# Requesting the modulation's weights from ScalarE's queue instead of SyncE's in a two-layer encoder kernel

## Chip, cores and metric

The kernel runs on one core of a Trainium2 chip. The metric is the device time of one launch in microseconds (us). The core has five engines with an instruction queue each: TensorE (PE; its weight loads are listed as PEld), VectorE (DVE), ScalarE (ACT), GpSimd (POOL) and SyncE (SP). Sixteen DMA engines move data between the memory outside the core and the on-chip buffers; an instruction on SP, ACT or POOL asks for a transfer.

## The reference

The program computes one inference step of a trunk of two layers on 384 rows of 2048 numbers: 256 rows of one new stream and 16 rows of each of 8 running streams. Each layer first makes three vectors for each of the 9 streams from a conditioning vector `c`. This is the **modulation**; its weights are a matrix of 2048 by 6144 for each layer, all in float32:

```
def modulate(x, c, norm_g, w_mod, b_mod):
    mod = jax.nn.silu(c) @ w_mod + b_mod
    shift, scale, gate = jnp.split(mod, 3, axis=-1)
    h = rms_norm(x, norm_g) * (1 + scale[:, None, :]) + shift[:, None, :]
    return h, gate[:, None, :]
...
    for l in range(DEPTH):
        h, gate = modulate(x, c, norm_g[l], w_mod[l], b_mod[l])
        ...  # even layer: spatial gating beside retention; odd layer: gated linear attention
        x = x + gate * y
```

The shift and scale of a layer are wanted before the layer's projections, its gate only after them. So of the modulation the kernel needs one third before anything of the first layer can start (shift and scale of layer 0 are two of six equal parts), and the other four parts (gate of layer 0; shift, scale and gate of layer 1) much later.

## The kernel before

**Granules.** Every big product is done in float32 accuracy with three products of a high and a low part. Weights come in granules of 256 by 512 numbers (512 KB). A granule goes through four hands: SP asks for it (`load_main`, line 391) into one of four `raw` buffers; ACT copies its high part to `whi` (`split_main`, line 775, the instruction at line 783); DVE subtracts to get the low part `wlo` (line 1133); PE multiplies it with three tiles of rows (`granule`, line 1715), which is 18 matmuls. ACT's `split_main(n)` waits until PE is through with granule n - 4 (the semaphore `w_used`, which starts at `LEAD` = 16), because there are four `whi` and `wlo` buffers. SP's `load_main(n)` waits until DVE has made the low part of granule n - 4 (`lo_ready`).

**The stretch that the change touches.** Granules 0 to 127 belong to the spatial gating of layer 0: four heads of 24 granules (three panels of 8: v, u and z) and, after each two heads, four output panels of 4 granules. Granules from 128 on belong to retention and to layer 1 and are loaded by another function (`load`, line 377, its DMA at line 389).

**The modulation's later parts.** Four parts (`GROUP`, i = 0 to 3) of 16 batches each make 64 batches, numbered `nb` from 32 on (0 to 31 are the first stage, `load_batch`, line 400). A batch is two transfers of 512 KB into one of two buffers (`SLOT` is 1 or 2 in turn; the buffers are the four `state` tiles, which the retention uses later). PE takes batches in pairs at 32 **places** between granules (`PLACE`, `group_batch`, line 1777: eight matmuls a batch in the trace, named `turn<-state,cT`, and one count on `mod_used`). A place lies behind some granule N: behind the 4th and 8th granule of a panel (every four granules), in one panel, the z panel of head 0, behind every second, and behind the last granule of each output panel. The table `BEHIND` says at which granule's load the pair for a place is asked for, two granules after N:

```
BEHIND[ph * (N_GM // 2) + 24 * (h % 2) + 8 * p + g + 2] += [nb, nb + 1]
...
BEHIND[min(ph * (N_GM // 2) + 48 + 4 * pn + 5, N_GM - 1)] += [nb, nb + 1]
```

In the kernel before, SP walks this table in `load_main`: behind its request for granule n it calls `load_group(nb)` (line 412, DMA at line 419) for the pair listed there. `load_group` waits on `mod_used` until PE has used the batch that was last in the same buffer, so until the place before, and everything later on SP's queue waits behind it. SP's requests are all on one hardware DMA queue (q1 in the profile); POOL's are on another (q0).

Of the kernel before, what the change touches and what calls it, by code (L numbers as in the profile page):

```python
# [34 lines left out]
W = 512  # L35
# [16 lines left out]
N_GM = 128  # L52
# [5 lines left out]
GROUP = [(0, 8), (1, 0), (1, 4), (1, 8)]  # L58
# [3 lines left out]
BEHIND = {n: [] for n in range(N_GM)}  # L62
for ph in range(2):
    for h in (2 * ph, 2 * ph + 1):
        for p in range(3):
            for g in ((), (3, 7), (1, 3, 5, 7))[IN_HEAD[h][p] // 4]:
                nb = NBATCH * N_FIRST + 2 * len(PLACE)
                PLACE["head", h, p, g] = (nb, nb + 1)
                BEHIND[ph * (N_GM // 2) + 24 * (h % 2) + 8 * p + g + 2] += [nb, nb + 1]
    for pn in range(4):  # L70
        nb = NBATCH * N_FIRST + 2 * len(PLACE)
        PLACE["out", ph, pn] = (nb, nb + 1)
        BEHIND[min(ph * (N_GM // 2) + 48 + 4 * pn + 5, N_GM - 1)] += [nb, nb + 1]
SLOT = [nb % 5 if nb < NBATCH * N_FIRST else 1 + nb % 2 for nb in range(N_BATCH)]
TURN = [SLOT[:nb].count(SLOT[nb]) for nb in range(N_BATCH)]
LAST = [max([-1] + [n for n in range(nb) if SLOT[n] == SLOT[nb]]) for nb in range(N_BATCH)]
# [13 lines left out]
def build(nc, a, consts, outs):  # L90
# [6 lines left out]
    w_m = [a["w_mod"][l].rearrange("(k p) n -> p k n", p=P) for l in range(2)]  # L97
# [4 lines left out]
    with ExitStack() as ctx:  # L102
# [6 lines left out]
        def sem(name):  # L109
            return ctx.enter_context(nc.semaphore(name))  # L110
# [30 lines left out]
        def carve(at, *shape):  # L141

            v = work[:, at:at + int(np.prod(shape))]
            if len(shape) == 2:
                v = v.rearrange("p (a b) -> p a b", a=shape[0])
            if len(shape) == 3:
                v = v.rearrange("p (a b c) -> p a b c", a=shape[0], b=shape[1])
            return v
# [7 lines left out]
        MT = [(raw[1][:, :, :], raw[3][:, :, :])] + [  # L156
            tuple(state[c][:, :].rearrange("p (k n) -> p k n", k=GK) for c in (2 * i, 2 * i + 1)) for i in range(2)] + [
            (carve(1536, GK, W), carve(3584, GK, W)), (carve(4608, GK, W), carve(5760, GK, W))]
# [64 lines left out]
        s = {n: sem(n) for n in names}  # L223
# [3 lines left out]
        mod_in = [sem(f"mod_in{k}") for k in range(len(MT))]  # L227
# [3 lines left out]
        def at_least(eng, sm, n):  # L231

            if not isinstance(n, int) or n > 0:
                eng.wait_ge(sm, n)
# [16 lines left out]
        def main_slot(n):  # L251

            return n - N_GM if n >= N_GM else (1, 3, 0, 2)[n % 4] if n >= 8 else 2 * (n % 2)

        def main_raw(n):

            return raw[main_slot(n)][:, :, :]

        def main_turn(n):

            return sum(main_slot(m) == main_slot(n) for m in range(n + 1))

        def group_of(nb):

            return (nb - NBATCH * N_FIRST) // KT, (nb - NBATCH * N_FIRST) % KT
# [92 lines left out]
        def nothing(*_):  # L358
            pass
# [16 lines left out]
        def _(sp):  # L376
# [14 lines left out]
            def load_main(n, src):  # L391

                if n in (8, 9):
                    sp.wait_ge(s["mod_used"], max(nb for nb in range(N_FIRST * NBATCH) if SLOT[nb] == 0) + 1)
                else:
                    at_least(sp, s["lo_ready"], n - 1 if n < 8 else n - 3)
                sp.dma_start(main_raw(n), src).then_inc(main_in[main_slot(n)], 16)
                for nb in BEHIND[n]:
                    load_group(nb)

            def load_batch(q, b):

                nb, p = NBATCH * q + b, PANEL[q]
                at_least(sp, s["mod_used"], LAST[nb] + 1)
                if nb == 3:
                    sp.wait_ge(s["cT_full"], 1)
                for i in range(2):
                    k = 4 * b + 2 * i
                    sp.dma_start(MT[SLOT[nb]][i], w_m[0][:, k:k + GK, p * W:p * W + W])\
                        .then_inc(mod_in[SLOT[nb]], 16)  # L410

            def load_group(nb):

                i, k = group_of(nb)
                layer, p = GROUP[i]
                sp.wait_ge(s["mod_used"], LAST[nb] + 1)
                for q in range(2):
                    c0 = (p + 2 * q) * W
                    sp.dma_start(MT[SLOT[nb]][q], w_m[layer][:, k, c0:c0 + 2 * W].rearrange("p (j n) -> p j n", j=2))\
                        .then_inc(mod_in[SLOT[nb]], 16)  # L420

            def panel(r, src):
# [8 lines left out]
            def gmlp_main(h, n0, p, g):  # L431
                c0 = (D, 0, 2 * D)[p] + h * W
                load_main(n0 + 8 * p + g, w_e[:, GK * g:GK * g + GK, c0:c0 + W])

            def modulation():
                for m in range(8):
                    for b in range(NBATCH):
                        if m % 2 == 0 and m >= 2 and b == 3:
                            gmlp_main(0, 0, 0, m - 2)
                        if m % 2 and m >= 3 and b == 1:  # L440
                            gmlp_main(0, 0, 0, m - 2)
                        load_batch(m, b)
# [6 lines left out]
            def gm_out(ph, pn, n, ai, yi, oi, before):  # L449
                for g in range(4):  # L450
                    k = ph * 8 + GK * g
                    load_main(n + g, wo[0][:, k:k + GK, pn * W:pn * W + W])
# [309 lines left out]
        def _(act):  # L762
# [12 lines left out]
            def split_main(n):  # L775

                if n >= N_GM:
                    act.wait_ge(raw_in[n - N_GM], 32)
                else:
                    act.wait_ge(main_in[main_slot(n)], 16 * main_turn(n))  # L780
                if n >= NSLOT:
                    act.wait_ge(s["w_used"], n - NSLOT + 1 + LEAD)
                act.activation(whi[n % NSLOT][:, :, :], main_raw(n), ACT.Copy).then_inc(s["hi_ready"], 1)  # L783

            def start():
                act.wait_ge(s["cT_full"], 1)
                act.activation(cth, SC[:, 0:KT * NC9].rearrange("p (k c) -> p k c", k=KT), ACT.Tanh,
                               scale=0.5).then_inc(s["th_done"], 1)
                act.wait_ge(s["vec_full"], 1)
                act.activation(vecT, OB[0][:, 0:P], ACT.Copy).then_inc(s["vec_done"], 1)  # L790
# [29 lines left out]
            def modulation():  # L820
                panel_out(0)
                for m in range(2, 8):
                    k0 = 4 * (m // 2 - 1)
                    if m % 2 == 0:
                        panel_out(m - 1)
                        act.wait_ge(s["sel_done"], m)
                        for k in (k0, k0 + 1, k0 + 2):
                            prompt(0, k)
                            high(0, k)
                        if m in (4, 6):  # L830
                            act.wait_ge(s["wsT_full"], m // 2 - 1)
                            act.activation(wsT_all[:, :, m // 2 - 2, :],
                                           OB[0][:, :].rearrange("p (h t) -> p h t", h=A_HEADS),
                                           ACT.Copy).then_inc(s["wsT_done"], 1)
                        panel_out(m)
                        split_main(m - 2)
                    else:
                        prompt(0, k0 + 3)
                        high(0, k0 + 3)
                        split_main(m - 2)  # L840
                panel_out(7)
                act.wait_ge(s["sel_done"], 8)
                for g in (6, 7):
                    prompt(0, 2 * g)
                    prompt(0, 2 * g + 1)
                    high(0, 2 * g)
                    high(0, 2 * g + 1)
                    split_main(g)
# [1457 lines left out]
```

## Time and profile before

| | |
|---|---|
| Median of 3 runs | 2734.3 us (2734.03 to 2734.69) |
| The profiled execution | 2733.85 us, of which the span of the trace is 2732.3 us |
| PE busy | 2674.1 us (98% of the span) |
| DVE, ACT, POOL busy | 1277.0, 880.1, 522.9 us |
| Mean DMA rate | 192 GB/s |
| TensorE clock granted | 0.992 of full speed (below it only near the start) |

The page has the busy time of each engine, the span in 40 slices, the DMA queues, the chain of work that ended last, and the costliest groups of instructions. Other views of the trace list who waited for whom, the instructions in order of time, and the time from a DMA's issue to its landing. Times inside the trace count from the span's start.

### The profile page before, as it was taken

Reading aid. Unit: us, or ns where it says so; the run is one execution under the profiler, and the core shown is the slowest. Engines: PE = TensorE matmul, PEld = TensorE weight load, DVE = VectorE, ACT = ScalarE, POOL = GpSimd, SP = SyncE. Lnnn points to the kernel's source line nnn. Section 1 sums busy time; section 2 is a strip of 40 time slices with the busy share of each in tenths; the row PEclk is TensorE's granted clock in tenths of the full one; section 3 lists DMA queues with packets and bytes.
Section 4 is the critical chain, followed back from the end, with each engine's and each line's share of the span. In section 5 each row is a group of like instructions: output and inputs, shape, how many; then the busy total and the mean of one; then the engine's idle time right before and its main releaser. Section 6 shows DMA issues by size and latency. Waiting matters only on the chain.

```text
span 2732.3 us, 36512 instructions
## 1 busy us (share of the span) xinstructions
PE 2674.1 (98%) x13257; PEld 2059.0 (75%) x13257; DVE 1277.0 (47%) x1849; ACT 880.1 (32%) x1241; POOL 522.9 (19%) x622
## 2 busy tenths in 40 slices
PE   6999999999999999999999999999999999999998
PEld 3677777777788888888877777786868777786866
DVE  2334343334444545455555464544554463544656
ACT  1423222222222332232323534422434334422431
POOL 3201030002311103111123121231122120231113
PEclk8999999999999999999999999999999999999999
DMA  9867676667654446455554364545556364655454
GB/s 374 316 247 260 227 252 226 228 215 235 217 178 143 157 158 211 129 173 179 169 161 126 101 231 144 199 150 185 163 182 195 117 230 140 203 159 185 157 190 154
DMA packets 280707, 523.78 MB, mean 192 GB/s; under 512 B 26593, under 2 KB 125041, under 8 KB 280041
## 3 DMA queue, kind: packets, MB, share of 16 engines
q1 hardware_dynamic: 240498, 389.17, 43.1%
q0 software_dynamic: 40064, 132.69, 14.2%
q8 instruction: 90, 1.47, 0.2%
q14 instruction: 55, 0.45, 0.1%
HBM read 460.78 MB, written 60.96 MB: 191 GB/s over the span
## 4 chain that ended last, share of the span: by engine, by line
PE 90%; issue 3%; DMA 2%; DVE 2%; POOL 1%; ACT 1%; SPq 0%; DVEq 0%; POOLq 0%; ACTq 0%
PE acc L1713 76%; PE turn L1713 6%; PE scores L1713 3%; PE mixed L1713 3%; DMA work<-in_w_mod 1%; DMA state<-in_w_mod 1%; POOL work L571 1%; DVE state L1665 1%; PE turn L1880 0%; DMA raw<-in_w_in_e 0%; POOL small L534 0%; POOL out L656 0%; PE mixed L1880 0%; PE turn L2120 0%; PE turn L2033 0%
## 5 line engine op out<-in xcount | busy, mean ns | idle before, releaser
L1713 PE MATMUL acc<-whi,hT_hi 128*128 128x512 f32 x2496 | 988.2, 396 | 5.8 <-POOL hT_lo L709 1.8
L1713 PE MATMUL acc<-whi,hT_lo 128*128 128x512 f32 x2496 | 973.6, 390 | 0.0
L1713 PE MATMUL acc<-wlo,hT_hi 128*128 128x512 f32 x2496 | 973.3, 390 | 0.0
L1122 DVE TENSOR_TENSOR wlo<-raw,whi 128x1024 fp32r<-128x1024 f32 x413 | 524.1, 1277 | 602.7 <-ACT whi L769 602.2
L769 ACT ACTIVATE whi<-raw 128x1024 fp32r<-128x1024 f32 x413 | 435.8, 1059 | 922.2 <-PE acc L1713 908.4
L1713 PEld LDWEIGHTS acc<-whi,hT_hi 128*128 128x128 f32 x2496 | 469.2, 188 | 153.0 <-issue 51.0
L1713 PEld LDWEIGHTS acc<-whi,hT_lo 128*128 128x128 f32 x2496 | 469.0, 188 | 100.3
L1713 PEld LDWEIGHTS acc<-wlo,hT_hi 128*128 128x128 f32 x2496 | 469.5, 188 | 93.2
L1133 DVE TENSOR_TENSOR wlo<-raw,whi 128x1024 fp32r<-128x1024 f32 x131 | 166.7, 1277 | 318.5 <-ACT whi L783 317.6
L1713 PE MATMUL acc<-whi,yT_hi 128*128 128x512 f32 x768 | 301.7, 393 | 7.1 <-DVE work L1381 3.7
L1713 PE MATMUL acc<-wlo,yT_hi 128*128 128x512 f32 x768 | 299.8, 390 | 0.0
L1713 PE MATMUL acc<-whi,yT_lo 128*128 128x512 f32 x768 | 299.5, 390 | 0.0
L783 ACT ACTIVATE whi<-raw 128x1024 fp32r<-128x1024 f32 x131 | 137.3, 1057 | 328.5 <-PE acc L1713 272.2
L617 POOL TENSOR_TENSOR x<-x,work 128x512 f32 (+1 forms) x90 | 140.0, 1581 | 316.5 <-DVE work L1381 311.1
L1713 PEld LDWEIGHTS acc<-whi,yT_hi 128*128 128x128 f32 x768 | 144.4, 188 | 46.3 <-issue 7.6
L1713 PEld LDWEIGHTS acc<-whi,yT_lo 128*128 128x128 f32 x768 | 144.6, 188 | 30.5
L1713 PEld LDWEIGHTS acc<-wlo,yT_hi 128*128 128x128 f32 x768 | 144.6, 188 | 29.6
L571 POOL TENSOR_TENSOR work<-work 128x512 f32<-128x512 f32 (+1 forms) x54 | 76.3, 1431 | 261.7 <-DVE work L1292 244.7
L1665 DVE SCALAR_TENSOR_TENSOR state<-state,work,turn 128x512 f32<-128x512 f32 x64 | 45.0, 745 | 168.2 <-PE mixed L1713 168.2
L656 POOL DMA_DIRECT2D out<-state x96 | 71.6, 745 | 180.3 <-DVE state L1665 146.3
L1713 PE MATMUL mixed<-work 32*128 32x512 f32 (+3 forms) x320 | 99.9, 530 | 0.0
L1713 PE MATMUL turn<-work 32*128 32x256 f32 (+3 forms) x384 | 98.1, 508 | 0.0
(241 smaller groups left out, 1784.6 us busy)
## 6 DMA issues: line engine op xcount, KB each, us to landing
raw<-in_w_in_o SPq DMA_DIRECT2D x384, 256.0 KB, 3.1
state<-in_w_mod SPq DMA_DIRECT2D x154, 512.0 KB, 5.9
raw<-in_w_in_e SPq DMA_DIRECT2D x256, 256.0 KB, 3.0
raw<-in_w_in_e SPq DMA_DIRECT2D x96, 512.0 KB, 7.1
out<-state POOLq DMA_DIRECT2D x96, 512.0 KB, 3.8
state<-in_state_gla POOLq DMA_DIRECT2D x64, 512.0 KB, 5.8
raw<-in_w_out_o SPq DMA_DIRECT2D x128, 256.0 KB, 3.5
raw<-in_w_out_e SPq DMA_DIRECT2D x32, 512.0 KB, 7.2
```

The lines of the kernel that those rows point to most:

```text
L571: pool.tensor_tensor(y[:, t, :], y[:, t, :], gate_tile(t), ALU.mult).then_inc(s["y_done"], 1)
L617: pool.tensor_tensor(xs, xs, out_tmp[kind][:, t, :], ALU.add).then_inc(s["x_added"], 1)
L656: pool.dma_start(piece(dst, h, c), state[c % NST][:, :].rearrange("p (b v) -> p b v", b=n))\
L769: act.activation(whi[jj][:, :, :], raw[jj][:, :, :], ACT.Copy).then_inc(s["hi_ready"], 1)
L783: act.activation(whi[n % NSLOT][:, :, :], main_raw(n), ACT.Copy).then_inc(s["hi_ready"], 1)
L1122: dve.tensor_tensor(wlo[jj][:, :, :], raw[jj][:, :, :], whi[jj][:, :, :].bitcast(F32), ALU.subtract).then_inc(s["lo_ready"], 1)
L1133: dve.tensor_tensor(wlo[j][:, :, :], main_raw(n), whi[j][:, :, :].bitcast(F32), ALU.subtract).then_inc(s["lo_ready"], 1)
L1665: dve.scalar_tensor_tensor(out=half, in0=half, scalar=eb[:, c // 4, b:b + 1], in1=up_bank(c, i)[:, :], op0=ALU.mult, op1=ALU.add)\
L1713: return pe.matmul(out, lhsT, rhs, start=start, stop=stop, skip_group_check=True)
```

## The change

SP's `load_main` no longer walks `BEHIND`. ACT's `split_main` does: behind the split of granule n it calls `load_group(nb)` for the same batches, and the wait on `mod_used` and the two transfers of each batch are now ACT's. The table, the buffers, the transfers, PE's places and the semaphores stay the same. The modulation's first stage (`load_batch`) stays on SP.

```diff
@@ load_main, on SP
                 sp.dma_start(main_raw(n), src).then_inc(main_in[main_slot(n)], 16)
-                for nb in BEHIND[n]:
-                    load_group(nb)
@@ on SP
-            def load_group(nb):
-
-                i, k = group_of(nb)
-                layer, p = GROUP[i]
-                sp.wait_ge(s["mod_used"], LAST[nb] + 1)
-                for q in range(2):
-                    c0 = (p + 2 * q) * W
-                    sp.dma_start(MT[SLOT[nb]][q], w_m[layer][:, k, c0:c0 + 2 * W].rearrange("p (j n) -> p j n", j=2))\
                         .then_inc(mod_in[SLOT[nb]], 16)
@@ split_main, on ACT
                 act.activation(whi[n % NSLOT][:, :, :], main_raw(n), ACT.Copy).then_inc(s["hi_ready"], 1)
+                if n < N_GM:
+                    for nb in BEHIND[n]:
+                        load_group(nb)
+
+            def load_group(nb):
+
+                i, k = group_of(nb)
+                layer, p = GROUP[i]
+                act.wait_ge(s["mod_used"], LAST[nb] + 1)
+                for q in range(2):
+                    c0 = (p + 2 * q) * W
+                    act.dma_start(MT[SLOT[nb]][q], w_m[layer][:, k, c0:c0 + 2 * W].rearrange("p (j n) -> p j n", j=2))\
+                        .then_inc(mod_in[SLOT[nb]], 16)
```

## Rows read from the trace of the kernel before

**Rows 1.** The page: busy time by engine, and the chain that ended last.
```profile
PE 2674.1 (98%) x13257; PEld 2059.0 (75%) x13257; DVE 1277.0 (47%) x1849; ACT 880.1 (32%) x1241; POOL 522.9 (19%) x622
...
PE 90%; issue 3%; DMA 2%; DVE 2%; POOL 1%; ACT 1%; SPq 0%; DVEq 0%; POOLq 0%; ACTq 0%
```

**Rows 2.** Waits of all engines, 125 to 700 us: total, times, longest.
```profile
ACT whi L783 <- PE acc L1713: 272.2, 77, 7.7
...
PEld turn L1713 <- issue: 30.7, 93, 0.8
...
PEld acc L1713 <- DVE wlo L1133: 0.8, 1, 0.8
```

**Rows 3.** Waits on SP's own queue, whole run: total, times, longest.
```profile
SPq L419 <- PE turn L1713: 229.2, 31, 15.4
```

**Rows 4.** Timeline of ACT, 670 to 692 us: start, length, instruction, idle before.
```profile
676.82 1.06 ACT L783 ACTIVATE whi<-raw 128x1024 fp32r<-128x1024 f32 x1 [3.02 <-PE acc L1713]
680.90 1.06 ACT L783 ACTIVATE whi<-raw 128x1024 fp32r<-128x1024 f32 x1 [3.02 <-PE acc L1713]
```

**Rows 5.** Timeline of PE around 685 us, with a pair's 16 matmuls.
```profile
684.50 0.39 PE L1713 MATMUL acc<-whi,yT_lo 128*128 128x512 f32 x1
684.81 1.92 PE L1713 MATMUL turn<-state,cT 128*32 128x512 f32 x16
```

**Rows 6.** Line 419, four issues a window, 128, 667 and 686 us; first lines: durations, first and last start.
```profile
L419 SPq DMA_DIRECT2D state<-in_w_mod x4: 432/450/502, 128.2 to 129.8; - x4
...
DMA to landing us min/median/max: 5.9/7.3/8.5
...
L419 SPq DMA_DIRECT2D state<-in_w_mod x4: 341/432/433, 667.5 to 668.8; - x4
...
DMA to landing us min/median/max: 3.7/5.1/6.5
...
L419 SPq DMA_DIRECT2D state<-in_w_mod x4: 341/431/919, 685.9 to 687.8; - x4
...
DMA to landing us min/median/max: 3.7/6.7/8.6
```

**Rows 7.** ACT's sequencer at line 782, and ACT's timeline, 164 us.
```profile
L782 ACTq EVENT_SEMAPHORE  x2: 17/17/17, 164.4 to 164.5; - x2
...
164.37 0.60 ACT L883 ACTIVATE work<-acc 128x512 f32<-128x512 f32 x1 [0.76 <-PE acc L1713]
```

**Rows 8.** Timeline of POOL from 645 us.
```profile
647.03 4.77 POOL L617 TENSOR_TENSOR x<-x,work 128x512 f32<-128x512 f32 x3 [6.37 <-DVE work L1381]
651.74 0.56 POOL L594 DMA_DIRECT2D work<-gate_rows  x1
```

**Rows 9.** Line 397, the one issue at 656.6 us: a granule's load.
```profile
DMA to landing us min/median/max: 9.3/9.3/9.3
```

**Rows 10.** A stretch: us; busy of PE, PEld, DVE, ACT, POOL; clock, DMA share, GB/s.
```profile
670.00:674.00 4.00, 4.00 (x19) 3.32 (x18) 0.17 (x1) 1.06 (x1) 1.87 (x3) 1.00 1.01 401
```

**Rows 11.** Timeline of DVE from 676 us.
```profile
677.91 1.23 DVE L1133 TENSOR_TENSOR wlo<-raw,whi 128x1024 fp32r<-128x1024 f32 x1 [2.85 <-ACT whi L783]
```

**Rows 12.** Line 419 at 199 us, and the pair's matmuls that follow.
```profile
L419 SPq DMA_DIRECT2D state<-in_w_mod x4: 340/432/433, 198.8 to 200.1; - x4
...
DMA to landing us min/median/max: 3.8/5.0/6.2
...
207.92 1.92 PE L1713 MATMUL turn<-state,cT 128*32 128x512 f32 x16
```

**Rows 13.** Timeline of PE at 186 us: the mixing ahead of a pair.
```profile
185.59 1.02 PE L1713 MATMUL mixed<-work 128*128 128x512 f32 x2
...
187.40 1.92 PE L1713 MATMUL turn<-state,cT 128*32 128x512 f32 x16
```

**Rows 14.** Timelines of ACT and PE at the hand-over to granule 128.
```profile
700.72 1.06 ACT L783 ACTIVATE whi<-raw 128x1024 fp32r<-128x1024 f32 x1 [14.69 <-DMA raw<-in_w_in_e]
...
706.62 0.47 PE L1713 MATMUL acc<-whi,hT_hi 128*128 128x512 f32 x1 [1.44 <-DVE work L1381]
```

More of the change, by code:

```diff
@@ L409, in load_batch @@
                     sp.dma_start(MT[SLOT[nb]][i], w_m[0][:, k:k + GK, p * W:p * W + W])\
-                        .then_inc(mod_in[SLOT[nb]], 16)
-            def load_group(nb):
-                i, k = group_of(nb)
-                layer, p = GROUP[i]
-                sp.wait_ge(s["mod_used"], LAST[nb] + 1)
-                for q in range(2):
-                    c0 = (p + 2 * q) * W
-                    sp.dma_start(MT[SLOT[nb]][q], w_m[layer][:, k, c0:c0 + 2 * W].rearrange("p (j n) -> p j n", j=2))\
                         .then_inc(mod_in[SLOT[nb]], 16)
```

## The prediction, written before the result was known

> **What bounds the kernel now.** I read the page first. PE is busy 98% of the span, and 90% of the chain that ended last is PE's own work [rows 1]. So the time changes only by what makes PE stand still or lets it stop standing still. The change touches the stretch from about 125 to 705 us (granules 8 to 127), so the next view is the list of waits there. ACT's idle time ahead of its splits is mostly time in which it waits for PE, the four `whi` buffers being full: 272.2 us [rows 2]. That is the normal state: ACT starts the split of granule n as PE ends granule n - 4. The pairs' matmuls (`turn<-state,cT`) never wait for their weights in this stretch: the row for them shows only the engine's own issue gaps, 0.8 us at most, 93 of them, which is under three for each of the 32 places, and no row names the DMA of `in_w_mod` [rows 2]. SP, however, stands 229.2 us in `load_group`'s wait, 31 times, up to 15.4 us [rows 3]. The reader should see both halves: SP is blocked for a long time, and because it is, it asks for the next pair the moment PE has used the last one. That early request is what the change gives up.
>
> **What is removed.** SP's 229.2 us of waiting and its four issues at each of 32 places (one such set goes from 667.5 to 668.8 us by its starts, with 0.43 us for the last [rows 6]). Both are idle time or issue time of an engine off the path, so they are worth what they cost PE. The trace shows two such costs. Once in the stretch PE's weight load waited 0.8 us for a low part that came late [rows 2]. And at the hand-over to granule 128 ACT waited 14.69 us for a granule which SP had asked for only behind the last pair; the slack of three granules ate nearly all of it, and PE stood 1.44 us [rows 14]. With SP free, the granules' loads depend on `lo_ready` alone and both go. Gain: 0.8 + 1.4 = 2.2 us.
>
> **What is moved: when a pair is asked for.** Take the pair at 684.81 us, behind granule N = 123 [rows 5]. Before, its four transfers were asked for from 667.5 us [rows 6], 17.3 us ahead. Now they stand behind the split of granule N + 2 = 125. The split that begins at 684.98 us follows PE's end of granule 123 and is that of 127, so the one at 676.82 us is 125's [rows 4]. From there to the pair is 7.99 us: two granules of 4.08 us, which is the distance of the splits [rows 4]. The second batch of the pair is wanted half of the pair's 16 matmuls later; they begin within about 1.3 us, so 0.7 us later. **Time available: 8.7 us.** The first batch's two transfers stand ahead of the second's, so the second decides.
>
> **What the four transfers take.** From the first issue to the last landing it is the distance of the first and last start plus the longest landing: 1.3 + 6.5 = 7.8 us at 667 us, but 1.6 + 8.5 = 10.1 us for the first set and 1.9 + 8.6 = 10.5 us for the last [rows 6]. Read in the same way, the 32 sets run from 7.5 to 10.8 us with a mean of 8.8 us; half of them are over 8.6 us. Behind 17.3 us this was free; behind 8.7 us it is not.
>
> **When ACT issues.** No row shows ACT issuing a DMA. One end: its sequencer goes on while the engine works, as at 164.4 us, where it took the two semaphore waits of line 782 during a 0.60 us activation that began at 164.37 us [rows 7]. Then the first issue comes some 0.1 us behind the start of the split. The other end: POOL's `gate_rows` DMA at 651.74 us starts as its tensor work ends (647.03 + 4.77 us [rows 8]); then ACT would issue behind its 1.06 us split [rows 4]. I take 0.1 us, since the row of ACT's own sequencer is the nearer. The four issues are priced like SP's. The wait on `mod_used` costs nothing where places are four granules apart, since the place before is two granules back. What stands behind it on ACT is the next split, due 4.08 us later; four issues of about 0.45 us are over by then, so neither DVE nor PE sees ACT late.
>
> **What the granules' loads now do to a pair.** Before, SP's queue held the pair ahead of the next granules. Now the granule loads come on another queue at the same time. SP asks for one when DVE has made a low part, at 677.91 + 1.23 us = 2.3 us behind the start of the split [rows 11], and then every 4.08 us. Its 512 KB take 1.3 us of the 401 GB/s which the DMA engines moved while loads were queued, their share being full [rows 10]. The lower end is 0 (the pair's packets go first); for the upper end the nearest row is a granule's load that ran beside POOL's `gate_rows` transfers and landed after 9.3 us instead of about 3.7 us [rows 6, 9], so up to 5.6 us. I take 1.3 us, one granule's bytes, because the interfering transfer is of that size and falls wholly within the pair's.
>
> The Trainium skill bears on this choice: its page "DMA: Bandwidth & Descriptors", section "Queues, rings and completion order", says that each DMA engine serves the queues that have work for it in turn, a packet at a time. By that rule the granule's load is through before the pair's is and adds its whole 1.3 us; by the order of one queue, as SP's requests stand now, it would add nothing and the sum below would be +11 us instead of +34 us. No row of this case shows two hardware queues side by side.
>
> **The sum.** A plain place is late by 0.1 + 8.8 + 1.3 - 8.7 = 1.5 us. Of the 32 places I count 24 as plain. Four (the z panel's fourth granule of each head, where the mixing stands ahead of the pair) have at least 1.8 us more [rows 13] and cost nothing. Three in the z panel of head 0 lie two granules apart; there both kernels must wait for `mod_used` and ask at the same moment, and the row of one such set lands its last at 200.1 + 6.2 = 206.3 us for a second batch wanted at 207.92 + 0.7 us [rows 12]: 2.3 us to spare, more than 1.3. The last place is asked for four granules ahead. So 24 x 1.5 = 36 us of new PE idle time, less 2.2 us: +34 us. The profiled execution took 2733.85 us (span 2732.3 us and 1.55 us around it), 0.45 us under the median of 2734.3 us; on the median the sum is 2768 us.
>
> **The ends.** If a granule's load adds nothing, the sets over 8.6 us alone are late, 0.57 us on the mean over the 32: 24 x 0.57 = 14 us, less 2.2: 2746 us; were every set as quick as 7.8 us, nothing would be late and only the gain stays: 2732 us. If ACT issues behind its split, each plain place loses 1.0 us more, 60 us in all, and the four with mixing about 0.7 us each: 2795 us. If two granules' loads fall into a pair's transfer (the second is asked for 6.4 us behind the split), 24 x 2.8 = 67 us: 2799 us. At 5.6 us a place 24 x 5.8 = 139 us, 2871 us; I give that almost nothing, since those `gate_rows` transfers are POOL's, of another shape.
>
> **Rivals.** *A. Not slower: the pair still lands in time.* Place: each pair's second batch. Price: 2732 us. It decides when the set's time and what the granule adds stay under 8.6 us together. For it: the sets at 7.5 to 7.8 us (eleven of 32), and a pair's rows may win over a granule's. Against it: half of the sets are already over that with nothing beside them but what was there before. Chance 0.17, of which 0.14 within 0.2% (5.5 us, about what a measurement can tell here) and 0.03 just above.
> *B. Later still: ACT issues when the split is done, or two granules' loads interfere.* 2785 to 2830 us. For it: POOL's row [rows 8]. Against it: ACT's sequencer row [rows 7]. Chance 0.27.
> *C. Faster: freed loads give PE back more than 2.2 us.* It would take over 5.5 us of idle PE time in the stretch that late granules cause, with pairs in time; the waits name 0.8 us and 1.44 us only [rows 2, 14]. About 2727 us. Chance 0.06.
>
> **How the numbers follow.** The forecast (pairs late by about 0.7 to 2.3 us at the plain places, 2748 to 2785 us) has 0.50 and is the likeliest: 2768 us. The range must leave out no more than 0.2: 2734 to 2800 us leaves out C, the lower third of A, and the upper third of B. Faster 0.06, same 0.14, slower 0.80.
>
> **What would show it.** After the change PE's first or second half of a pair should wait for the DMA of `in_w_mod` at some 24 places, 1 to 2 us each, in the list of waits; SP should have no waits on `mod_used` past the first stage; ACT's waits for granule loads and PE's 1.44 us at granule 128 should go. ACT's four issues should begin within 0.2 us of a split's start; if they begin 1.06 us behind it, B holds. If no pair waits, A holds, and the set's time from first issue to last landing will be under 8.6 us. The prediction is wrong if the four transfers on a queue of their own land quicker than SP's did, or if PE's waits at the pairs come with new waits for granules.

## The result, and the profile after

The changed kernel takes 2791.11 us (median of 4 runs, 2787.94 to 2796.66) beside 2734.49 us (4 runs, 2734.03 to 2735.49) for the kernel before: a ratio of 1.0206 [1.0193, 1.0218], so 57 us more. The forecast was 2768 us, 34 us more. The profiled execution of the changed kernel took 2796.66 us.

The page of the changed kernel, its parts on busy time, queues, the chain and the DMA issues:

```profile
PE 2687.0 (96%) x13257; PEld 2061.9 (74%) x13257; DVE 1275.3 (46%) x1849; ACT 879.9 (31%) x1241; POOL 521.8 (19%) x622
...
q1 hardware_dynamic: 222066, 322.05, 35.7%
...
q10 hardware_dynamic: 18432, 67.12, 7.2%
...
PE 80%; DMA 11%; issue 3%; DVE 2%; POOL 1%; ACT 1%; ACTq 1%; DVEq 0%; POOLq 0%; SPq 0%
...
state<-in_w_mod ACTq DMA_DIRECT2D x128, 512.0 KB, 6.9
```

PE's instructions are the same in number [rows 1]; the span grew by 62.8 us and PE's busy time by only 12.9 us, so some 50 us of the growth is idle PE. The 67 MB on q10 are the pairs: ACT's requests run on a hardware queue of their own beside SP's q1. In the chain DMA rose from 2% [rows 1] to 11%. That is not the loss itself: the chain counts a transfer from its request on, work that ran beside it included. The list of waits has what PE lost, here for the changed kernel from 125 to 770 us (total, times, longest):

```profile
ACT whi L771 <- PE acc L1714: 375.0, 89, 9.7
...
PEld turn L1714 <- DMA state<-in_w_mod: 70.1, 28, 3.8
PE turn L1714 <- DMA state<-in_w_mod: 46.3, 25, 2.9
...
PEld acc L1714 <- DVE wlo L1134: 7.5, 9, 0.8
ACT whi L771 <- DMA raw<-in_w_in_e: 4.7, 1, 4.7
```

The two rows with the DMA of `in_w_mod` are the new ones; [rows 2] has no such row. Of the two, PE's own is the loss: 25 waits, 46.3 us. PEld's are longer because weights are loaded ahead of the matmuls. SP's own queue in the same stretch:

```profile
SPq L397 <- DVE wlo L1134: 558.7, 116, 11.3
SPq L389 <- DVE wlo L1134: 29.8, 5, 17.5
```

SP's wait on `mod_used` [rows 3] is gone; it waits only for low parts, as its granules' requests need. So the change does what it says. One place shows what it costs. ACT's timeline around the split at 246.53 us, then line 783 (the pair's four issues there), SP's granule requests (line 397), and PE's timeline at the pair:

```profile
246.53 1.06 ACT L771 ACTIVATE whi<-raw 128x1024 fp32r<-128x1024 f32 x1 [2.68 <-PE acc L1714]
246.56 1.85 ACTq L783 DMA_DIRECT2D state<-in_w_mod  x4
```
```profile
L783 ACTq DMA_DIRECT2D state<-in_w_mod x4: 334/450/520, 246.6 to 247.9; - x4
...
DMA to landing us min/median/max: 5.6/7.7/10.3
```
```profile
L397 SPq DMA_DIRECT2D raw<-in_w_in_e x2: 368/368/368, 245.1 to 248.9; - x2
```
```profile
254.53 1.07 PE L1714 MATMUL turn<-state,cT 128*32 128x512 f32 x8
258.27 1.77 PE L1714 MATMUL turn<-state,cT 128*32 128x512 f32 x8 [2.68 <-DMA state<-in_w_mod]
```

The first issue stands 0.03 us behind the start of a split that takes 1.06 us: ACT does not wait for its own activation. The pair begins 8.0 us behind the split, as worked out. Its first eight matmuls run on time, its second eight wait 2.68 us: the second batch is late. From the first issue to the last landing the set took 11.7 us (1.3 + 10.3 with the starts unrounded), and two granule loads lie beside it: one asked for 1.4 us ahead of the pair, one 2.3 us behind. Read in this way, the 32 sets took 11.0 us in the mean (7.5 to 14.6); before it was 8.8 us. The lateness of the second batches is read from the distance of a pair's first and ninth matmul, less the 0.88 us that it has where nothing waits: 50.9 us at 25 places, 2.0 us each. It is a little more than the 46.3 us of waits, which count from the modelled end of the eighth matmul.

The set at 739 us is the exception that shows why. SP asks for no granule there between 727.7 and 745.6 us:

```profile
L783 ACTq DMA_DIRECT2D state<-in_w_mod x4: 334/448/456, 739.2 to 740.5; - x4
...
DMA to landing us min/median/max: 3.8/5.1/6.2
```

With no granule's load beside it until its last 1.1 us the set took 1.3 + 6.2 = 7.5 us and its pair didn't wait. This one set on ACT's queue is as quick as SP's quickest, 7.5 us.

The hand-over to granule 128 has no wait any more [rows 14], in PE's timeline:

```profile
765.57 1.92 PE L1714 MATMUL turn<-state,cT 128*32 128x512 f32 x16
767.42 0.50 PE L1714 MATMUL acc<-whi,hT_hi 128*128 128x512 f32 x1
```

Last, PE's 12.9 us of added busy time. Below 2.4 GHz the same matmul takes longer, and in this trace the granted clock fell to 0.50 (1.2 GHz) eight times between 149 and 733 us. Two of the eight stretches, with their sum over all eight (columns: stretch, length, busy time of PE, PEld, DVE, ACT, POOL, then the clock, the DMA share and GB/s), and PE's timeline ahead of the first:

```profile
149.30:152.70 3.40, 3.40 (x11) 2.48 (x8) 0.00 (x0) 0.00 (x0) 0.00 (x0) 0.50 0.68 255
...
729.50:732.90 3.40, 3.40 (x9) 2.66 (x9) 0.00 (x0) 0.00 (x0) 0.42 (x1) 0.50 0.70 245
sum 27.20, PE 26.71 PEld 17.18 DVE 4.87 ACT 0.00 POOL 6.98; mean PE 3.34 PEld 2.15 DVE 0.61 ACT 0.00 POOL 0.87
```
```profile
145.06 1.06 PE L1714 MATMUL turn<-state,cT 128*32 128x512 f32 x8
148.49 1.22 PE L1714 MATMUL turn<-state,cT 128*32 128x512 f32 x8 [2.36 <-DMA state<-in_w_mod]
149.64 0.80 PE L1714 MATMUL acc<-whi,hT_hi 128*128 128x512 f32 x1
```

PE had stood 2.36 us for a second batch, and 0.8 us later the clock was half. 27.2 us at half speed are 13.6 us lost. For the profiled execution the account closes: 50.9 + 13.6 - 2.2 (the gain as predicted) = 62.3 us, or 63.1 us with only the 1.4 us of that gain that PE's own waits show, against 2796.66 - 2733.85 = 62.8 us.

### The profile page after: what moved, and what is told of

The parts are those of the page before. It is cut to its first block, busy times and chain, and to the rows that moved or that the text cites. A ratio compares the mean times of both kernels' runs of the same rounds, so it can differ in the third digit from the quotient of the medians.

```text
span 2795.1 us, 36512 instructions
## 1 busy us (share of the span) xinstructions
PE 2687.0 (96%) x13257; PEld 2061.9 (74%) x13257; DVE 1275.3 (46%) x1849; ACT 879.9 (31%) x1241; POOL 521.8 (19%) x622
## 4 chain that ended last, share of the span: by engine, by line
PE 80%; DMA 11%; issue 3%; DVE 2%; POOL 1%; ACT 1%; ACTq 1%; DVEq 0%; POOLq 0%; SPq 0%
PE acc L1714 67%; DMA state<-in_w_mod 9%; PE turn L1714 5%; PE scores L1714 3%; PE mixed L1714 3%; ACTq L783 1%; DMA work<-in_w_mod 1%; POOL work L559 1%; DVE state L1666 0%; PE turn L1881 0%; ACT whi L771 0%; POOL small L522 0%; DMA work<-gate_rows 0%; POOL out L644 0%; PE turn L2034 0%
## 5 line engine op out<-in xcount | busy, mean ns | idle before, releaser
L1714 PE MATMUL turn<-state,cT 128*32 128x512 f32 x616 | 85.2, 636 | 58.5 <-DMA state<-in_w_mod 58.5
```

The source lines that it names most:

```text
L1714: return pe.matmul(out, lhsT, rhs, start=start, stop=stop, skip_group_check=True)
```

## The experiments

Theory T: a pair is late because it is asked for later, and because the granule loads on the other queue lengthen its transfer. Rivals: that ACT's queue or ACT's part in it is slower by itself; that only the later moment matters and SP would lose the same; that the waits cost little and the fallen clock makes the difference. "N + 2" is the granule behind whose split a pair is asked for, as in [rows 4] for N = 123; PE takes the pair behind granule N.

**The moment of the request, on ACT's queue.** Three kernels shift the table by a constant. Nothing else is changed:

```diff
-  BEHIND[ph * (N_GM // 2) + 24 * (h % 2) + 8 * p + g + 2] += [nb, nb + 1]
+  BEHIND[ph * (N_GM // 2) + 24 * (h % 2) + 8 * p + g + 0] += [nb, nb + 1]   # e1; + 1 in e2, + 3 in e4
-  BEHIND[min(ph * (N_GM // 2) + 48 + 4 * pn + 5, N_GM - 1)] += [nb, nb + 1]
+  BEHIND[min(ph * (N_GM // 2) + 48 + 4 * pn + 3, N_GM - 1)] += [nb, nb + 1] # e1; + 4 in e2, + 6 in e4
```

N + 0, some 8 us earlier:

> Each pair is still asked for on ScalarE's queue, but behind the split of granule N (two granules earlier than in the changed kernel), so as soon as the pair before is used. Theory moment (the pairs are asked for too late, 8.7 us ahead for a set of four transfers that took about 10.9 us): no pair waits, the eight short drops of TensorE's clock inside the stretch go, and the hand-over stays repaired: 2730 to 2736 us. Theory queue (ScalarE's queue or its issuing is what costs): the sets stay long and ScalarE now also waits up to 6 us in places: still 2770 us or more.

N + 1, some 4 us earlier:

> Behind the split of granule N + 1: one granule earlier than in the changed kernel, 12.8 us ahead of the second batch. Theory moment: sets of 9.5 to 12.8 us just fit, a few of the longest are late by up to 1 us: 2731 to 2740 us. Theory queue: 2770 us or more.

N + 3, some 4 us later:

> Behind the split of granule N + 3: one granule later than in the changed kernel, 4.6 us ahead of the second batch. Theory moment: each plain place is late by some 4 to 6 us instead of 2, and the z panel of head 0 and the four places with mixing are late too; with more drops of the clock 2870 to 2940 us. Theory queue: the moment matters little, 2780 to 2820 us.

| asked for behind the split of | time, us (before 2735.23) | ratio | mean set, us | second batch late |
|---|---|---|---|---|
| N + 0 (e1) | 2735.10 | 1.0 [0.9991, 1.0009] | 9.9 | never |
| N + 1 (e2) | 2735.98 | 1.0 [0.9991, 1.0009] | 10.3 | 2 places, 2.3 us in all |
| N + 2 (the change) | 2791.11 (before 2734.49) | 1.0206 [1.0193, 1.0218] | 11.0 | 25 places, 50.9 us |
| N + 3 (e4) | 2978.31 | 1.0896 [1.0879, 1.0913] | 9.8 | both batches late |

The waits of N + 1 from 125 to 770 us, and those of N + 3 from 125 to 950 us:

```profile
PEld turn L1714 <- DMA state<-in_w_mod: 4.4, 3, 1.9
PE turn L1714 <- DMA state<-in_w_mod: 1.9, 2, 1.0
```
```profile
PEld turn L1714 <- DMA state<-in_w_mod: 207.2, 57, 5.7
PE turn L1714 <- DMA state<-in_w_mod: 164.5, 60, 5.3
```

One granule (4.08 us) earlier is enough for nearly all, although the sets there still take 10.3 us. So with the request early enough, ACT as the issuer and the freed SP cost nothing and give nothing that this measurement can tell. Whether ACT's queue is itself slower these two runs don't show, since the earlier request would hide it; the runs with held loads below test that. One granule later leaves 8.7 - 4.1 = 4.6 us for a set of 9.8 us: with all 32 places taken alike 32 x 5.2 = 166 us, and PE's waits are 164.5 us. The loss is larger, 243 us, and the time over the 2940 us that was the upper end given for it. The rest is in the page of N + 3:

```profile
PE 2751.0 (92%) x13257; PEld 2082.0 (70%) x13257; DVE 1276.1 (43%) x1849; ACT 881.1 (30%) x1241; POOL 521.6 (18%) x622
```

PE does the same 13257 matmuls in 76.9 us more than before [rows 1], and 164.5 + 76.9 = 241.4 us, as much as that execution was longer (2976.5 - 2735.23 = 241.3 us). In its trace the granted clock fell to 1.2 GHz in 30 stretches with 215 us between 125 and 950 us; over the span it is 0.958 instead of 0.989. So here the waits bring with them a fallen clock that costs some 77 us.

N + 0 has one cost of its own. In the dense z panel of head 0 the place before is two granules back, so ACT's wait on `mod_used` at N + 0 ends late, and the evictions of `acc` stand behind it on ACT. Its row in the waits:

```profile
PE acc L1714 <- ACT work L884: 1.8, 1, 1.8
```

The sixth kernel keeps N + 0 but asks at N + 2 for the place at g = 1, which removes that row:

```diff
-  BEHIND[ph * (N_GM // 2) + 24 * (h % 2) + 8 * p + g + 0] += [nb, nb + 1]
+  BEHIND[ph * (N_GM // 2) + 24 * (h % 2) + 8 * p + g + (2 if g == 1 else 0)] += [nb, nb + 1]
```

> As the first experiment (pairs asked for behind the split of granule N), but the one place behind the second granule of head 0's z panel stays at N + 2, where the first experiment held ScalarE up ahead of an eviction for which TensorE then waited 1.78 us. 1.8 us under the first experiment: 2732 to 2735 us. If that wait was hidden elsewhere: the same as the first experiment.

It took 2734.38 us beside 2735.92 us, 0.9995 [0.9986, 1.0004]. The wait is gone; a gain of 1.5 us is inside the interval and so not shown.

**The same lateness on SP's queue.** The kernel before, with its request for a pair held back on SP until about the moment at which ACT asks in the changed kernel:

```diff
                 sp.dma_start(main_raw(n), src).then_inc(main_in[main_slot(n)], 16)
+                if BEHIND[n] and n < N_GM - 1:
+                    sp.wait_ge(s["w_used"], n - NSLOT + 1 + LEAD)
                 for nb in BEHIND[n]:
                     load_group(nb)
```

> SyncE keeps the pairs on its own queue, ahead of the next granules' loads, but waits until TensorE is through with granule N - 2, the moment at which the changed kernel asks. Theory interference (the granule loads that run beside a pair on another queue make a set 10.9 us instead of 8.8): sets of 7.5 to 9.5 us against 8.7 us, late by 0.2 to 0.6 us on the mean, 2742 to 2755 us. If the moment alone makes the loss and the second queue nothing: sets of about 10.9 us again, 2780 to 2795 us.

2765.75 us, 1.0117 [1.0101, 1.0132], which is more than was expected of it, and not for the pairs' sake. Its waits from 125 to 950 us, and SP's own from 125 to 770 us:

```profile
ACT whi L785 <- DMA raw<-in_w_in_e: 146.0, 42, 10.4
...
PEld acc L1715 <- DVE wlo L1135: 31.3, 9, 5.8
PE acc L1715 <- DVE work L1383: 23.4, 7, 4.9
...
PE turn L1715 <- DMA state<-in_w_mod: 1.3, 2, 0.8
```
```profile
SPq L421 <- PE acc L1715: 279.1, 27, 15.5
```

The pairs come in time (1.3 us of waits) since their sets take 8.3 us in the mean: on one queue the next granules' loads stand behind them. In exchange SP is blocked for 279.1 us in the new wait, ACT waits 146 us for granules, and PE waits at the low parts and at the output panels; its trace also has five stretches at 1.2 GHz, 17 us in all. So a late request costs on either queue, but in other places: on one queue the granules pay for the pair, on two the pair pays for the granules. That the sets differ, 8.3 us here and 11.0 us in the change, speaks for T's second half, but this run changed more than the queue.

**Holding the granule loads back.** This tests the second half alone. ACT asks as in the change, but SP doesn't send a granule's load until the pair has landed; in the first kernel the load that comes behind the pair, and with it what stands behind that on SP's queue; in the second the one just ahead of the pair too. The wait is on the counts of the pair's landing:

```diff
 # load_main, on SP, ahead of the request for granule n
+  for nb in BEHIND[n - NSLOT] if n - NSLOT < N_GM - 1 and n >= 8 else ():    # e5; BEHIND[n - 3] in e8
+      sp.wait_ge(mod_in[SLOT[nb]], 32 * TURN[nb] + 32)
```

> The changed kernel, but SyncE asks for granule N + 6 (the first one that would be asked for while the pair for the place behind granule N is under way) only when that pair has landed. Queue, moment and issue of the pairs are those of the changed kernel; only the granule loads beside them are gone. Theory interference: sets of 7.5 to 9 us instead of about 11, pairs late by 0.5 us or less, 2738 to 2755 us. If ScalarE's queue is itself slower than SyncE's: sets stay at 10 us or more and the time over 2775 us.

> As the run with SyncE's hold, but granule N + 5 is held back too, the one that is asked for 1.7 us ahead of a pair. Theory interference with two granules' loads, each adding its own 1.3 us: sets of 7.5 to 8.7 us with first transfers landing after 3.8 us instead of 4.9, hardly a pair late, 2735 to 2743 us. If ScalarE's queue makes the rest of the difference: sets stay at 9.6 us on the mean and the time at 2750 to 2756 us.

One load held: 2753.52 us beside 2735.92 us, 1.0065 [1.005, 1.0081]. Both held: 2741.52 us beside 2735.06 us, 1.0023 [1.0014, 1.0032]. The waits of the two kernels for pairs, 125 to 950 us; then, of the second, the same place as above (there at 242 us, its pair at 250 us) and its SP requests between 236 and 256 us:

```profile
PE turn L1716 <- DMA state<-in_w_mod: 15.8, 17, 2.6
```
```profile
PE turn L1716 <- DMA state<-in_w_mod: 6.9, 8, 1.6
```
```profile
L785 ACTq DMA_DIRECT2D state<-in_w_mod x4: 334/448/456, 242.1 to 243.5; - x4
...
DMA to landing us min/median/max: 3.8/6.0/7.4
```
```profile
L399 SPq DMA_DIRECT2D raw<-in_w_in_e x3: 368/368/469, 251.0 to 253.0; - x3
```

The mean set falls from 11.0 to 9.8 and to 9.0 us, PE's waits from 46.3 to 15.8 and 6.9 us, and the loss from 57 to 18 and 6 us. At the place shown, the set took 8.7 us instead of 11.7 with SP's loads moved to 251 us, and its pair didn't wait. The moment of the request was not touched. At the 24 plain places alone the mean sets are 11.0, 9.7 and 8.6 us (8.8 us before). So ACT's queue is not slower by itself, and some 50 of the 57 us need both: the later request and the granule loads beside it. Both times are in their expected ranges; the first kernel's sets, 9.8 us, are over the 7.5 to 9 us expected, and the second's 9.0 us a little over 8.7 us. SP stands long for this (324.4 us in the first of the two kernels), and PE doesn't feel it: the granules have that much slack.

**What the fallen clock costs.** Eight matmuls whose result nobody uses stand between the two batches of 22 pairs, so that PE doesn't stand still there; nothing else is changed. The extra work only adds:

```diff
+  def fill():
+      for _ in range(8):
+          mm(T[1][:, 0:NTOK], hT[0][:, 0, 0:P], hT[0][:, 1, :])
...
+  if nb % 2 and (p < 2 or h and g == 7) and (h, p, g) not in ((2, 0, 3), (3, 1, 3)):
+      fill()      # ahead of a pair's second batch; likewise at seven of the output panels
   group_batch(nb)
```

> The changed kernel with eight more matmuls (some 1.4 us, into a PSUM bank that nobody reads then) between the two batches of 22 pairs, where TensorE otherwise stands and waits some 2 us for the second batch. Theory clock (the eight drops of the granted clock follow TensorE's standing still and cost 12 to 14 us of the loss beside the waits): the drops go or get rare and the time falls to 2776 to 2784 us, though TensorE does more. If the waits alone make the loss: 2790 to 2796 us.

2785.82 us, 1.0192 [1.0176, 1.0207], between the two ranges, so it decides nothing. It was run again beside the changed kernel on one chip:

> The changed kernel once more, beside the next one on the same chip, to price the clock: 2787 to 2794 us.

> The filled kernel once more. If the drops of the granted clock cost 12 to 14 us, it is 10 us or more under the changed kernel; if a drop's cost is mostly taken back by a shorter wait for the pair that comes next, 3 to 7 us under it; if the clock costs nothing, within 2 us of it or above.

The changed kernel again: 2794.02 us (2784.56 to 2798.04), 1.0211 [1.0196, 1.0227]. With the fill: 2788.71 us (2786.3 to 2792.43), 1.0196 [1.0182, 1.021]. PE's waits for pairs with the fill (first run, 125 to 770 us), and the fallen stretches of the changed kernel's second trace, their sum last:

```profile
PE turn L1714 <- DMA state<-in_w_mod: 8.5, 12, 1.8
```
```profile
695.50:702.30 6.80, 6.13 (x18) 3.60 (x19) 2.11 (x3) 0.00 (x0) 5.63 (x5) 0.50 0.52 160
sum 13.60, PE 12.93 PEld 8.07 DVE 2.11 ACT 0.00 POOL 5.63; mean PE 4.31 PEld 2.69 DVE 0.70 ACT 0.00 POOL 1.88
```

The fill takes the falls away (none in the first run's trace, one in the second's, from 125 to 770 us), while the sets stay as long (10.6 and 10.8 us) and the pairs as late (47.5 and 51.0 us, most of it now covered by work without use). It gives back 5.3 us in the pair of medians from one chip, the middle one of the three answers named for it, and 6.7 us in the first pair, each beside its own kernel before (56.6 and 49.9 us more); not the 12 to 14 us that the eight falls of the first trace had suggested. The second trace of the changed kernel tells why: it has three fallen stretches with 13.6 us, which is 6.8 us lost, and its account is 47.2 + 6.8 - 2.2 = 51.8 us against 49.5 us measured for that execution. The number of falls changes from one execution to the next. The intervals with and without the fill overlap: if the fill itself costs nothing, the price of the clock lies between nothing and (1.0227 - 1.0182) x 2735 = 12 us of the 57, and which it is stays open; the rest is lateness.

No kernel of these is faster than the kernel before by more than the measurement can tell; the best, N + 0 but for one place, has the whole of its 1.5 us inside its interval.

## Why the forecast fell short

**Right.** PE bounds the kernel, and the pairs' waits are the main effect: 25 places, 46.3 us. The second batch decides, never the first. The time available was nearly right: 7.97 us from the request to the pair at most plain places, then 0.88 us instead of 0.7 us to its second half. ACT asks 0.03 us behind the start of a split at 21 of the 24 plain places, so the row of its sequencer [rows 7] was the right one to go by and POOL's [rows 8] was not. Twenty-three of the 24 places counted as plain are late; the 24th is the quick set at 739 us. The hand-over's 1.44 us are gone. Its partner of 0.8 us is not: nine weight loads now wait up to 0.8 us for a low part, 7.5 us of PEld's time; PE's own waits have no row for it.

**The step that failed** is the term for a granule's load: "I take 1.3 us, one granule's bytes, because the interfering transfer is of that size and falls wholly within the pair's." The size of one load was right, the count was not: at least two lie in a pair's transfer. The second one was missed because the prediction looked only for requests behind the pair's. SP, now free, asks for a granule when DVE has made a low part, every 4.08 us; one such request lies 2.3 us behind the split, as predicted, and the one before it 1.8 us ahead at most places (1.4 us at the place shown), still under way when the pair's first packets are due. It shows in the first transfer, which landed after 4.8 us in the mean instead of 4.0 us; with the load behind held it still took 4.8 us, with the one ahead held too 4.1 us. Measured, the term is 11.0 - 8.8 = 2.2 us, which makes a place late by 0.03 + 8.8 + 2.2 - 8.7 = 2.3 us instead of 1.5, or 2.1 us with the 0.88 us; by the trace the plain places add up to 50.9 - 1.1 - 0.8 = 49 us (the two taken off are not plain) instead of 36, 2.1 us at each of the 23. Holding the loads back, first the one behind and then both, took 1.2 and 0.8 us off the mean set, which is the experiment that shows it.

The rule of the Trainium skill that was weighed there ("DMA: Bandwidth & Descriptors", section "Queues, rings and completion order": an engine serves its queues in turn, a packet at a time) agrees with these runs: at the plain places the load asked for just behind the pair adds 1.3 us and the one just ahead 1.1 us, about the 1.3 us of its bytes. The quick set at 739 us and the 8.3 us of the sets on one queue are its other side. The rule had to be applied to every load under way, not to the next one.

Two smaller terms. The dense z panel and the mixing places were put at nothing; one of each was late, by 1.1 and 0.8 us. And the price of the fallen clock was not in the sum at all: 13.6 us in the profiled execution, 6.8 us in the next one profiled, some 5 us by the medians and not clear of their noise.

**The rivals.** The measured 2791 us lies above the forecast's own range of 2748 to 2785 us and in rival B's, 2785 to 2830 us, which had a chance of 0.27. The outer range, 2734 to 2800 us, holds it only because it takes in that part of B. Of B's two causes the first (ACT issues behind its split) is refuted by the issue times; the second (two granules' loads interfere) is what happened, though by the load ahead, not by the one asked for 6.4 us behind the split. That third load does lie beside eleven of the late plain places' sets, but they take 11.1 us in the mean, and ten that have none 10.8 us. Rival A falls: no set beside granule loads was quick enough at a plain place. Rival C falls too: with the pairs in time (N + 0, N + 1) the freed SP gives nothing that can be measured.

## What to carry to other kernels

A request that moves to another engine's queue loses its place in the first queue's order: what used to stand behind it now runs beside it. Count every transfer that is under way from its issue to its landing, those asked for just ahead of it too, and add the bytes of each before comparing with the time at hand. If a load must move, move its request earlier by what it has lost: here one granule (4.08 us) turned 57 us into nothing that could be measured.

## What was not expected of the hardware

The granted clock fell at short idle times of PE. Between 82 and 1427 us the kernel before never left 2.4 GHz (it did at 1427 us and in the last 8 us, so not only near the start); the changed kernel, whose PE stands still for at most 2.9 us at a time, fell to 1.2 GHz eight times in one execution and three times in the next, each time behind such a wait or in its last 0.7 us, and other waits of 2.5 us had no fall behind them. With the pairs still late but PE fed with useless matmuls, the falls went from eight and three to none and one. At half clock consecutive matmuls of a granule start 0.43 us apart instead of 0.23 us.
